# A fused two-block layer on one core: decay differences on ScalarE, one forget-sum copy and one low part in other places

## What is computed

```python
x = x + g2[..., None, :] * rmsnorm(yx, post_ffn_g[i])      # end of block one ("post2")
xn = rmsnorm_2(h, attn_norm_w[i])                          # start of block two ("norm3")
proj = xn @ w_in[i]
g_qkv = jax.nn.silu(causal_depthwise_conv(g_qkv, conv_w[i]))
g_decay = -jnp.exp(a_log) * jax.nn.softplus(g_a + dt_bias)
gc = jnp.cumsum(g, axis=-1)
diff = gc[..., :, None] - gc[..., None, :]
decay = jnp.where(lower, jnp.exp(jnp.where(lower, diff, 0.0)), 0.0)
c = jnp.cumsum(log_f, axis=1)                              # forget sums of FoX
```

## Time and profile before

| what | value |
|---|---|
| median of three runs | 828.97 us (828.56 to 829.82) |
| the profiled execution | 829.55 us |
| its span | 827.6 us |
| mean granted clock of TensorE | 0.989 of full speed |
| TensorE busy | 789.4 us, 95% |
| VectorE busy | 509.3 us, 62% |
| ScalarE busy | 390.7 us, 47% |
| POOL busy | 96.5 us, 12% |

### The profile page before, as it was taken

How to read it: one execution, slowest core, us unless ns; L and a number is a source line. 1 busy time by engine, 2 the same in 40 slices (tenths; PEclk the granted TensorE clock), 3 DMA queues, 4 the chain that set the end, 5 groups by cost and what they waited for, 6 DMA issues and landing times. The chain is left out here.

```text
span 827.6 us, 12597 instructions
## 1 busy us (share of the span) xinstructions
PE 789.4 (95%) x5111; PEld 701.8 (85%) x5111; DVE 509.3 (62%) x660; ACT 390.7 (47%) x538; POOL 96.5 (12%) x154
## 2 busy tenths in 40 slices
PE   4899999999999999999989999999999999999996
PEld 3578787777799999987879997988889999998884
DVE  0375689867685766684568786554465455453465
ACT  2433413444675565443266645557363434434264
POOL 3010131401100000000061313210100000000000
PEclk9999999999999999999999999999999999999998
DMA  9946567733366555568527341231465655545611
GB/s 327 389 132 217 166 235 262 277 115 108 109 228 202 162 164 186 203 231 302 178 56 224 107 154 51 103 102 51 153 203 179 203 163 192 171 161 202 216 65 51
DMA packets 103804, 144.83 MB, mean 175 GB/s; under 512 B 6343, under 2 KB 62160, under 8 KB 103760
## 3 DMA queue, kind: packets, MB, share of 16 engines
q1 hardware_dynamic: 96416, 137.38, 49.6%
q10 hardware_dynamic: 7280, 6.83, 2.7%
q0 software_dynamic: 64, 0.01, 0.0%
HBM read 142.10 MB, written 2.10 MB: 174 GB/s over the span
## 5 line engine op out<-in xcount | busy, mean ns | idle before, releaser
L1909 PE MATMUL ps<-h_hi,w_hi 128*128 128x256 f32 x720 | 204.5, 284 | 0.2 <-DVE w_lo L1263 0.2
L1910 PE MATMUL ps<-h_lo,w_hi 128*128 128x256 f32 x720 | 203.7, 283 | 0.0
L1911 PE MATMUL ps<-h_hi,w_lo 128*128 128x256 f32 x720 | 203.7, 283 | 0.0
L1263 DVE TENSOR_TENSOR w_lo<-raw,w_hi 128x2048 fp32r<-128x2048 f32 (+1 forms) x61 | 135.3, 2225 | 62.0 <-ACT w_hi L663 61.7
L663 ACT CAST w_hi<-raw 128x2048 fp32r<-128x2048 f32 (+1 forms) x61 | 113.1, 1856 | 88.4 <-PE ps L1911 53.0
L1271 DVE TENSOR_TENSOR w_lo<-raw,w_hi 128x2048 fp32r<-128x2048 f32 x44 | 100.8, 2290 | 62.2 <-ACT w_hi L671 62.2
L1909 PEld LDWEIGHTS ps<-h_hi,w_hi 128*128 128x128 f32 x720 | 138.2, 192 | 0.5 <-DVE w_lo L1263 0.5
L1910 PEld LDWEIGHTS ps<-h_lo,w_hi 128*128 128x128 f32 x720 | 138.2, 192 | 0.0
L1911 PEld LDWEIGHTS ps<-h_hi,w_lo 128*128 128x128 f32 x720 | 138.2, 192 | 0.0
L671 ACT CAST w_hi<-raw 128x2048 fp32r<-128x2048 f32 x44 | 83.6, 1901 | 51.8 <-PE ps L1911 50.5
L1909 PE MATMUL ps<-w_hi,h_hi 128*128 128x512 f32 x184 | 74.8, 407 | 1.2 <-DVE h_lo L1289 0.7
(11 more groups left out here) (396 smaller groups left out, 1280.4 us busy)
## 6 DMA issues: line engine op xcount, KB each, us to landing
raw<-in_ffn_up_w SPq DMA_DIRECT2D x22, 1024.0 KB, 5.1
raw<-in_w_gate_up SPq DMA_DIRECT2D x22, 1024.0 KB, 5.1
raw<-in_ada_w SPq DMA_DIRECT2D x16, 1024.0 KB, 5.3
raw<-in_w_in SPq DMA_DIRECT2D x14, 1024.0 KB, 5.4
raw<-in_m_in_w SPq DMA_DIRECT2D x11, 1024.0 KB, 5.3
raw<-in_ffn_down_w SPq DMA_DIRECT2D x10, 1024.0 KB, 5.0
raw<-in_w_down SPq DMA_DIRECT2D x10, 1024.0 KB, 4.9
raw<-in_m_out_w SPq DMA_DIRECT2D x4, 1024.0 KB, 5.4
```

The lines of the kernel that those rows point to most:

```text
L1263: dve.tensor_tensor(part_view(w_lo, s), raw_view(split[s]), part_view(w_hi, s).bitcast(F32), ALU.subtract).then_inc(lo_ready, 1)
L1909: pe.matmul(dst, l_hi, r_hi, start=first, stop=False)
L1910: pe.matmul(dst, l_hi, r_lo, start=False, stop=False)
L1911: return pe.matmul(dst, l_lo, r_hi, start=False, stop=last)
```

## The change

Three things are done. First, the decay differences go from VectorE to ScalarE: relu(column - row) in eight ScalarE instructions, read from the banks of TensorE, and the exponential gets the scale -1. They wait for the column sums in `gc`. `p_store(1)` is written behind the exponentials instead of ahead of them. Second, `fsum_out(1)` goes ahead of the split of the group G0+6 and of `gdn_silu(3)`; it stood behind both and behind two squarings. Third, in `post_norm` of "post2", the low part of the group G0 was made behind the first half's diagonal; now it is made behind the second half's update of `x`, ahead of its diagonal. Other lines only follow from these.

```diff
             gdn_mid(1)
             gdn_mid(2, ahead=False)
-            p_store(1)
+            act.wait_ge(S("egc_diff"), 1)
             for t in range(TT):
-                act.wait_ge(S("dec_z"), t + 1)
+                act.wait_ge(S("decay_mm"), 1 + t + 1)
+                for h in range(GH):
+                    act.activation(decT[:, GH * t + h, :], ps[:, 5 + t, h * P:(h + 1) * P], ACT.Relu, bias=gc[:, t, h:h + 1],
+                                   scale=-1.0).then_inc(S("dec_z"), 1)
+            for t in range(TT):
+                act.wait_ge(S("dec_z"), GH * (t + 1))
                 d = decT[:, GH * t:GH * (t + 1), :]
-                act.activation(d, d, ACT.Exp).then_inc(S("dec_exp"), 1)
+                act.activation(d, d, ACT.Exp, scale=-1.0).then_inc(S("dec_exp"), 1)
             act.wait_ge(S("egc_diff"), 2)
             for i in (0, 2):
                 act.activation(egc[:, i, :], egc[:, i, :], ACT.Exp).then_inc(S("egc_exp"), 1)
+            p_store(1)
             gdn_silu(0)
             gdn_silu(1)
             fsum_out(0)
             hi_until(at["gdn"][2] + 4)
             gdn_silu(2)
-            gdn_mid(3)
+            gdn_mid(3, ahead=False)
+            fsum_out(1)
+            hi_until(at["gdn"][3] + 4)
             gdn_silu(3)
             act.wait_ge(S("p_stored"), 32)
             token_squares(0)
             token_squares(1)
-            fsum_out(1)
...
+                    before_diagonal(t)
                     diagonal(norm, t, base("rstd", post) + 2 * t + 2)
-                    if t == 0 and after_diagonal is not None:
-                        after_diagonal()
...
-            post_norm("post2", "norm3", gp2, (2, 6), after_diagonal=lambda: lo_until(at["gdn"][0] + 1))
+            post_norm("post2", "norm3", gp2, (2, 6), lambda t: lo_until(at["gdn"][0] + t))
...
-            for t in range(TT):
-                dve.wait_ge(S("decay_mm"), 1 + t + 1)
-                for h in range(GH):
-                    ins = dve.tensor_scalar(decT[:, GH * t + h, :], ps[:, 5 + t, h * P:(h + 1) * P], gc[:, t, h:h + 1], 0.0,
-                                            ALU.subtract, ALU.min)
-                    if h < GH - 1:
-                        link(ins)
-                ins.then_inc(S("dec_z"), 1)
```

More of the change, by code:

```diff
@@ L1301, in p_weights_lo, with post_norm @@
                 lo_part(pw_lo[:], pw_raw[n], pw_hi[:], "pw_step")
-            def post_norm(post, norm, gain, banks, before_diagonal=None, after_diagonal=None):
+            def post_norm(post, norm, gain, banks, before_diagonal):
                 def gained(n, t, count):
@@ L1319, in post_norm @@
                             .then_inc(S("x_upd"), 1)
-                    if t == 0 and before_diagonal is not None:
-                        before_diagonal()
+                    before_diagonal(t)
                     diagonal(norm, t, base("rstd", post) + 2 * t + 2)
-                    if t == 0 and after_diagonal is not None:
-                        after_diagonal()
             def ada1_rows(n):
@@ L1575, in _, with p_parts @@
             lo_until(at["mix_out"][1] + 3)
-            def p_parts():
+            def p_parts(t):
+                if t:
+                    return
                 dve.wait_ge(S("p_step"), 2)
@@ L2438, in _ @@
             gdn_tiles(3)
-            pe.wait_ge(S("dec_z"), TT)
+            pe.wait_ge(S("dec_z"), GH * TT)
             to_tokens(0, 0, TOKEN_BANKS[0])
```

## The result

| | before | changed |
|---|---|---|
| median of 15 runs | 828.28 us (826.43 to 829.82) | 830.97 us (828.93 to 832.16) |
| profiled execution | 829.55 us | 830.39 us |
| its span | 827.6 us | 828.7 us |
| mean granted clock in it | 0.989 | 0.992 |

The ratio is 1.0026, with a 95% interval of 1.0017 to 1.0036: the change costs 1.4 to 3.0 us. The forecast was 832.0 us in a range of 829.9 to 833.6, with 0.78 on slower.

The account below looks back on a forecast made before the run. TensorE, busy 95%, was taken as the bound, with ScalarE's and VectorE's chains setting its waits. 0.36 + 2.65 = +3.0 us gave 832.0 us for the median, range 829.9 to 833.6.

Parts of the forecast that it names:

- What bounds: TensorE busy 95% of the span, only its waits winnable; ScalarE and VectorE in 448 to 460 us decide the Silus.
- Part one, +2.65: Differences on ScalarE: the table load of Silu, and with it the four Silus, start 2.65 us later.
- rectifiers: Eight 128x128 relu instructions on ScalarE for the decay differences, taking 2.18 us.
- load: The exponential's table load on ScalarE, no longer covered by VectorE's work, adding 1.29 us.
- store: `p_store(1)` with its issue, now between the exponentials and Silu on ScalarE, adding 1.54 us.
- the exponentials: Two large exponentials at 0.54 us each and two short ones at 0.31 together, on ScalarE's path.
- VectorE's relief: VectorE loses 2.92 us of work but gains nothing, since its next convolution waits for `egc`.
- Part two: Bank 7 emptied earlier: TensorE's 1.11 us wait at the forget sums goes; worth at most 0.45 us at the `gT` products.
- Part three, +0.36: Second norm: POOL locked out behind the moved low part, so TensorE turns the second half 0.36 us later.
- The rival without a lock: Second norm: POOL not locked out, -0.72 in place of +0.36, total +1.9, 830.9 us; chance 0.09.
- The clock: TensorE's wait at 425 us grows to 2.7; a fall to 1.2 GHz there adds 1.5, 833.5 us; chance 0.10.
- The sum: 0.36 + 2.65 = +3.0 us on the profiled execution, 829.55 to 832.55; 832.0 us for the median.

Follow-up runs that it names:

- Part one alone: Kernel before with only the decay differences on ScalarE and `p_store(1)` behind the exponentials: 830.39 us, ratio 1.0024.
- part two alone: Kernel before with only `fsum_out(1)` moved ahead of the split of G0+6: 827.38 us, ratio 0.9986.
- both first: Changed kernel with `p_store(1)` and the two short exponentials of `egc`, with their table load, ahead of the rectifying instructions: 829.92 us, ratio 1.0010.
- part three alone: Kernel before with only the low part of G0 moved ahead of the second diagonal: 828.10 us, ratio 0.9991.
- load first: Changed kernel with the two short exponentials of `egc`, and their table load, ahead of the eight relu instructions: 831.93 us, ratio 1.0033.
- store first: Changed kernel with `p_store(1)` back ahead of the wait for `gc`, run twice: 830.36 us, ratio 1.0020; then 830.18 us, ratio 1.0010.
- early split: Kernel before with `fsum_out(1)` moved ahead and the split of G0+5 ahead of `p_store(1)` and the exponentials: 827.87 us, ratio 0.9998.
- mask later: Changed kernel with POOL's memset of the masks waiting until the second diagonal is written: 831.07 us, ratio 1.0031.
- norm only: Kernel before with G0's low part in two halves, ahead of and behind the second diagonal, and POOL's memset behind that diagonal: 827.42 us, ratio 0.9982.
- the last kernel: Kernel before with `fsum_out(1)` and G0+5's split earlier, G0's low part halved, memset later, `p_store(1)` behind `gdn_tiles(3)`'s middle taps: 829.28 us, ratio 1.0005.

## Why the prediction was right, point by point

- **What bounds.** Right. ScalarE's chain to the Silus, and from the split of G0+5 VectorE's chain, set the `gT` products, and TensorE didn't. Part one alone and part two alone show it from both sides: TensorE late and the products unmoved, TensorE early and the products unmoved.
- **Part one, +2.65.** Measured +2.51 from the `egc` copy to the table load of Silu (3.95 before, 6.46 now). Term by term: copy of `egc` and signal 0.20 (0.22 forecast), rectifiers 2.20 (2.18), load 1.29 (1.29), store 1.52 (1.54). The mis-sized term is the exponentials: 1.25 for the four in a row (452.58 to 453.83), forecast 1.39. Nearly all of it is the two short ones: they took 0.31 before, when a table load stood behind them, and 0.19 here (453.64 to 453.83), where a copy begins before they end. The two large ones took 1.06 (1.08 forecast). The Trainium skill ("ScalarE: Activation LUTs", section "Rules for kernel authors") would have the minimum on VectorE. Here eight took 2.18 us on ScalarE and 2.92 on VectorE, and in the run with both first most of the delay goes by ScalarE's order alone, so no run here bears that rule out for a difference of this shape.
- **VectorE's relief is worth nothing.** Right: its 2.92 us less of work turned up as a wait of 4.84 us for `egc` where 0.89 had been.
- **Part two.** Right: the wait at the sums vanished. Where it would come back was half told: the wait before the `gT` products became 0.78 (0.9 forecast), but the larger share, 0.82, came back earlier, at the turns of `qk_n`, which VectorE feeds and where before there was no wait.
- **Part three, +0.36.** The turn came 0.35 later, by the chain as worked out: POOL at 420.98 held until 422.34, which is 0.17 behind the low part's end at 422.17, as in the earlier trace rows. The rival without a lock is out. But only 0.14 reached `h_hi`, and that is the step that failed. I let TensorE's time stand for all behind it. The first reader of the turned tokens is ScalarE, and it was held by its own queue before: there `h_hi` started at 425.96, and its last small load issue ran until 425.91. Timeline of ScalarE, before:

```profile
425.46 0.45 ACTq L674 DMA_DIRECT2D gprm<-in_fox_f_bias  x1
425.96 3.04 ACT L742 ACTIVATE h_hi<-ps,cols 128x256 fp32r<-128x256 f32 x8 [0.99 <-PE ps L2035]
```

  In the changed kernel the update comes 0.7 us earlier, the issues behind its squares too, and they end at 423.70, out of the way of `h_hi` at 424.66. So part of the gain that the prediction wrote off at POOL was paid out here. But the start of `h_hi` doesn't set the chain's start by itself. In part one alone its load issues ended late and it began at 9.66, 0.30 later than before, and still `egc` was copied at 33.62 as before. What made up for it is a small low part on VectorE. Part one alone (ScalarE, VectorE), then before (VectorE):

```profile
424.65 3.03 ACT L742 ACTIVATE h_hi<-ps,cols 128x256 fp32r<-128x256 f32 x8 [1.31 <-PE ps L2033]
429.70 0.29 DVE L1281 TENSOR_TENSOR wg_parts<-wsm,wg_parts 128x128 fp32r<-128x128 f32 x1 [0.95 <-ACT wg_parts L966]
...
431.02 0.56 DVE L1275 TENSOR_TENSOR wg_parts<-wsm,wg_parts 128x128 fp32r<-128x128 f32 x1 [0.96 <-ACT wg_parts L966]
```

  It took 0.56 before, and 0.29 both in part one alone and in the changed kernel. In the changed kernel the two low parts behind it gave these 0.27 back: 4.94 us from their start to the convolution, where it had been 4.67. That 0.11 is left at the chain's start is the sum of these; why they differ was not tested.
- **The clock.** The wait at 425 us grew to 2.70, and in the profiled execution there was no fall; it came in others (below).
- **The sum.** +3.0 forecast, +2.54 at the end of the trace, +2.15 in the ratio, 2.69 between the medians. From the 0.46 too much in the sum, 0.25 are part three's, 0.14 the exponentials', 0.07 were given back after the `gT` products. The base was 0.7 too high as well: 15 runs of before have the median 828.28. Both errors lie on the same side, and the forecast came 1.0 us above the measured median, inside the range.

## What to carry to other kernels

Before work goes to an engine that is "only 47% busy", look at what that engine does while it waits: here a table load and a store of 2.8 us in all had been hidden in a wait of 3.7 us, and 2.16 of the 2.51 us that part one cost came from these two having lost their cover. Put what needs no input ahead of the wait, what needs it behind, and count the room: two things that each fit may not fit together. A low part or any other long VectorE instruction with POOL's small ones beside it is best cut so that it doesn't lie over POOL's next instruction; and a wait that is gone from the bound's engine is only a gain if the next thing that it needs doesn't come from another chain.

## What the runs showed of the hardware

- **The place of a clock fall isn't fixed.** In six of the 14 profiles TensorE waited 2.70 or 2.71 us at the second turn. Behind it the clock stayed at 1.00 in four (changed, part three alone, load first, both first) and went to 0.69 and 0.66 over 425 to 430 us in two (store first, twice). It fell there also where the wait was 2.35 (early split) and 2.15 (mask later). All four profiles with a fall there had one over 380 to 390 us too. Of the ten without, two had one (before, and norm only, whose wait is 1.10). What links the two falls, these runs don't tell.
- **The spread of a kernel's runs is mostly this clock.** The runs of one kernel scatter by 0.8 to 1.9 us (standard deviation), and, in all kernels but one (part one alone, 0.8 and then 1.1), by 0.4 to 0.9 once they are brought to equal clock with the slope above. Comparing medians of 12 runs without it gave an order (load first slower than the changed kernel) that neither the `gT` products in the trace nor the number at equal clock bears out.
- **A write-only POOL instruction is enough to hold VectorE.** The memset, which reads nothing, stretched the diagonal from 0.28 to 0.84.
- **A store can hold the engine that issued it.** `p_store(1)` (128 x 2 x 512 numbers, 512 KB), issued at 458.28 in the last kernel, released ScalarE at 466.08, 7.8 us later; 4.34 us of these were idle.
